# Turning probability blocks ahead, summing head norms in four 32-row strips, and moving a convolution and a state load in a hybrid decoder step

## The reference

```python
x += 0.5 * swiglu(rmsnorm(x)); x += mixer(rmsnorm(x)); x += 0.5 * swiglu(rmsnorm(x))   # per layer
# layer 0, mixer = [forgetting attention, 4 heads of 128 | gated DeltaNet, 4 heads of 128]
s = q @ k.T * scale + c_i - c_j; p = softmax(causal(s)); o = p @ v            # prompt; samples read a paged cache
c = silu(causal_conv(u, w))              # 12 chunks of 128 channels: q 4, k 4, v 4; four taps
q = l2norm(q) * 128 ** -0.5; k = l2norm(k)                                    # per head, over its 128 channels
M = tril_strict(k_beta @ k.T * gam) + I; X = solve(M, [v_beta, k_beta * exp(gc)])
v_new = u - w @ S; o = (q * exp(gc)) @ S + (q @ k.T * gam) @ v_new; S = S * exp(gl) + k_dec.T @ v_new
o = rmsnorm(o) * silu(z)
# layer 1, mixer = retention, 8 heads of 128 x 256: rope, decayed attention in 4 chunks, a state per sample token
```

## Time and profile before

| | us |
|---|---|
| time of the three runs, median (lowest to highest) | 2624.53 (2623.72 to 2630.95) |
| the profiled execution, its own time | 2619.68 |
| its span, first to last instruction | 2617.9 |
| PE busy (95% of the span) | 2497.5 |
| POOL / DVE / ACT busy | 1682.8 / 1269.6 / 566.7 |
| mean granted TensorE clock | 0.977 |
| attention heads and convolution | about 620 to 690 |
| norm of q and k | about 690 to 715 |
| DeltaNet pairs | about 715 to 864 |
| closing norm and gate | about 864 to 897 |
| retention turns | about 1709 to 2116 |

### The profile page before, as it was taken

The page is one execution under the profiler, slowest core; times in us unless marked ns, Lnnn a source line. Parts: engine busy times, 40 slices in busy tenths (PEclk is TensorE's granted clock), DMA queues, the critical chain, the costliest instruction groups (busy, mean ns, idle before and its releaser), DMA issues.

```text
span 2617.9 us, 53417 instructions
## 1 busy us (share of the span) xinstructions
PE 2497.5 (95%) x20047; PEld 2395.9 (92%) x20047; DVE 1269.6 (48%) x2225; ACT 566.7 (22%) x847; POOL 1682.8 (64%) x750
## 2 busy tenths in 40 slices
PE   7999998997789899999999999999999899999997
PEld 7999998995467799999999999999889799999996
DVE  4444335786333564443344443366766644444433
ACT  3222101004633222220022220022222221222101
POOL 5777775663411377777777777765545457777773
PEclk9999999998789899999999999999999999999998
DMA  4333334894375333333323333233333423333331
GB/s 125 90 89 96 101 79 113 285 308 131 84 220 188 85 89 95 89 88 99 118 81 89 95 91 100 82 91 100 116 116 98 126 81 88 89 95 90 96 93 61
DMA packets 472390, 291.19 MB, mean 111 GB/s; under 512 B 32785, under 2 KB 438411, under 8 KB 472270
## 3 DMA queue, kind: packets, MB, share of 16 engines
q1 hardware_dynamic: 407286, 221.15, 29.0%
q10 hardware_dynamic: 64992, 68.54, 8.4%
HBM read 273.50 MB, written 16.23 MB: 111 GB/s over the span
## 4 chain that ended last, share of the span: by engine, by line
PE 83%; DVE 8%; ACT 3%; issue 3%; DMA 1%; POOL 1%; ACTq 1%; DVEq 0%; SPq 0%; POOLq 0%
PE ACC L799 72%; PE ACC L1055 2%; PE ACC L1028 1%; DVE TB L2261 1%; DMA SSR<-in_state_ret_S 1%; DVE SSR L2178 1%; POOL WLO L708 1%; PE ACC L1306 0%; PE ACC L1296 0%; DVE XL L1736 0%; PE ACC L1122 0%; PE ACC L1037 0%; POOL WHI L705 0%; PE ACC L893 0%; PE ACC L1330 0%
## 5 line engine op out<-in xcount | busy, mean ns | idle before, releaser
L705 POOL TENSOR_TENSOR WHI<-RAW,ZERO 128x1024 fp32r<-128x1024 f32 (+1 forms) x341 | 693.0, 2032 | 677.2 <-PE ACC L799 640.3
L708 POOL TENSOR_TENSOR WLO<-RAW,WHI 128x1024 fp32r<-128x1024 f32 (+1 forms) x341 | 915.5, 2685 | 49.3 <-POOL WHI L705 2.3
L799 PE MATMUL ACC<-XH,WHI 128*128 128x260 f32 x4032 | 822.6, 285 | 4.3 <-DVE XL L1736 2.0
L799 PE MATMUL ACC<-XH,WLO 128*128 128x260 f32 x4032 | 813.7, 283 | 0.0
L799 PE MATMUL ACC<-XL,WHI 128*128 128x260 f32 x4032 | 812.4, 283 | 0.0
L799 PEld LDWEIGHTS ACC<-XH,WHI 128*128 128x128 f32 x4032 | 624.8, 189 | 22.9 <-issue 6.5
L799 PEld LDWEIGHTS ACC<-XH,WLO 128*128 128x128 f32 x4032 | 622.9, 189 | 0.0
L799 PEld LDWEIGHTS ACC<-XL,WHI 128*128 128x128 f32 x4032 | 621.6, 189 | 0.0
L799 PE MATMUL ACC<-HH,WHI 128*128 128x260 f32 x1408 | 284.2, 283 | 1.1 <-POOL WLO L708 1.1
L799 PE MATMUL ACC<-HH,WLO 128*128 128x260 f32 x1408 | 283.1, 282 | 0.0
L799 PE MATMUL ACC<-HL,WHI 128*128 128x260 f32 x1408 | 282.6, 282 | 0.0
(11 more groups left out here) (391 smaller groups left out, 2398.7 us busy)
## 6 DMA issues: line engine op xcount, KB each, us to landing
RAW<-in_ffn_w_gu SPq DMA_DIRECT2D x176, 512.0 KB, 3.9
RAW<-in_ffn_w_down SPq DMA_DIRECT2D x64, 704.0 KB, 4.8
KPAGES<-in_cache_fox_k ACTq DMA_DIRECT2D x128, 256.0 KB, 4.1
RAW<-in_c_w_in SPq DMA_DIRECT2D x48, 512.0 KB, 3.9
VPAGES<-in_cache_fox_v SPq DMA_DIRECT2D x72, 256.0 KB, 3.1
RAW<-in_ab_w_in SPq DMA_DIRECT2D x28, 512.0 KB, 5.4
VPAGES<-in_cache_fox_v ACTq DMA_DIRECT2D x56, 256.0 KB, 3.3
SSR<-in_state_ret_S ACTq DMA_DIRECT2D x8, 1024.0 KB, 5.4
```

What stands on the lines that cost most here:

```text
L705: pool.tensor_tensor(WHI[:, slot, 0:nk, :], RAW[:, slot, 0:nk, :], ZERO[:, :].broadcast_to([P, nk, P]), ALU.add).then_inc(hi_split, 1)
L708: pool.tensor_tensor(WLO[:, slot, 0:nk, :], RAW[:, slot, 0:nk, :], WHI[:, slot, 0:nk, :].bitcast(F32), ALU.subtract).then_inc(split, 1)
L799: ins = pe.matmul(ACC[acc][:, n, 0:HALF], w[:, slot, k, :], a[:, k0 + k, n * HALF:(n + 1) * HALF], start=first and opens, stop=final and c ...
```

## The change

The diff does five things.

- **Heads.** PE turns blocks 0 and 1 of a head first, and then, behind the value product of block q, turns block q+2. The turn of the next head's keys stands ahead of the two turns, that of its values behind them. ACT moves the high part of head h-1 into head h, takes `exponent(h, 3)` at the head's start, and places its three `conv_taps` between the copies. DVE takes the low part of head h-1 and the first maximum of head h+1 ahead of `normalize(h, 3)`.
- **Value convolution.** Chunks 9 to 11 leave the last head and stand on ACT behind the root of the norm. Silu of v stands in the first DeltaNet pair behind the scaled keys, with its own semaphore `cv_value`, for which PE waits before it turns v; Silu of z stands behind the root of the closing norm, with `cv_gate`.
- **Norm sums.** Squares of q are taken by DVE, those of k by ACT in two parts. The sums go to one bank, each (q or k, half) in a strip of 32 rows by 260 columns; root and reciprocal work on 128 rows by 260 columns (RN); a broadcast reads one strip. Two `values()` stand ahead of the sums and two behind, in place of four behind. The closing norm goes the same way, its sums in the order of heads 0, 2, 1, 3.
- **First pair's end.** `value_sum(1)` stands ahead of `sample_gates`; PE takes both corner products ahead of the two `values()`.
- **Retention.** The load of SSR, with its wait for the store, stands ahead of `swap(1, "k")`.

```diff
-        fb_pe = Steps(sem("fb_pe"), [f"{w}{q}" for q in range(NBLK) for w in ("turn", "pv")])
+        fb_pe = Steps(sem("fb_pe"), [f"{w}{q}" for q, w in ((0, "turn"), (1, "turn"), (0, "pv"), (2, "turn"), (1, "pv"), (3, "turn"), (2, "pv"), (3, "pv"))])
...
             for h in range(FOX_HEADS):
-                if 0 < h < FOX_HEADS - 1:
-                    fox_tokens(h + 1)
+                later = 0 < h < FOX_HEADS - 1
+                if later:
+                    fox_token_turn(h + 1, AB_K, "ktok")
+                fox_turn(h, 0)
+                fox_turn(h, 1)
+                if later:
+                    fox_token_turn(h + 1, AB_V, "vtok")
                 for q in range(NBLK):
-                    fox_turn(h, q)
                     if h + 1 < FOX_HEADS:
                         score(h + 1, q)
...
                     fox_values(h, q)
-
-            pe.wait_ge(fb_dve.sem, fb_dve.value("lo", FOX_HEADS - 1))
+                    if q + 2 < NBLK:
+                        fox_turn(h, q + 2)
...
+            for _ in range(V_SLOTS // 2):
+                values()
             for j in range(2 * GDN_HEADS):
...
-                    ins = pe.matmul(ACC[0][0:NORM_ROWS, n, 0:HALF], row_select(r), SQH[:, j, n * HALF:(n + 1) * HALF],
-                                    start=j == 0, stop=j == 2 * GDN_HEADS - 1)
+                    ins = pe.matmul(bank(0)[strip(2 * (j // GDN_HEADS) + n), 0:HALF], row_select(j % GDN_HEADS), SQH[:, j, n * HALF:(n + 1) * HALF],
+                                    start=j % GDN_HEADS == 0, stop=j % GDN_HEADS == GDN_HEADS - 1)
             ln_pe.done(ins, "sum")
-            for _ in range(V_SLOTS):
+            for _ in range(V_SLOTS // 2):
                 values()
...
+                    rows, r = strip(2 * (j // GDN_HEADS) + n), 32 * (2 * (j // GDN_HEADS) + n) + j % GDN_HEADS
+                    ins = pe.matmul(ACC[1 + j % 2][:, n, 0:HALF], IDENT[rows, r:r + 1].broadcast_to([32, P]), RN[rows, :], start=True, stop=True)
...
                 values()
+                pe.wait_ge(cv_value, 1)
                 for q in range(2):
                     await_step(pe, gl_act, f"kde{q}", p)
                     turned(q, GV, f"vt{q}")
...
                 corner_xt(0)
+                corner_xt(1)
                 values()
-                corner_xt(1)
                 values()
...
+            for h in range(FOX_HEADS):
+                last = h == FOX_HEADS - 1
+                if h > 0:
+                    if not last:
+                        fox_query(h + 1)
+                    fox_high(h - 1)
+                    if not last:
+                        fox_keys(h + 1)
+                fox_turned(h, 0)
+                fox_turned(h, 1)
+                if h > 0:
+                    exponent(h, 3)
+                if not last:
+                    conv_taps(3 * h)
+                    fox_turned(h, 2)
+                    exponent(h + 1, 0)
+                    exponent(h + 1, 1)
+                    conv_taps(3 * h + 1)
+                    fox_turned(h, 3)
+                    exponent(h + 1, 2)
+                    conv_taps(3 * h + 2)
+                else:
+                    fox_turned(h, 2)
+                    fox_silu(0)
+                    fox_silu(1)
+                    fox_turned(h, 3)
+                    fox_silu(2)
+                    fox_silu(3)
+                    fox_high(h)
...
-            ln_act.done(act.activation(SQH[:, 0:GDN_HEADS, :], channels(GQ, GDN_HEADS), ACT.Square), "sqq")
-            ln_act.done(act.activation(SQH[:, GDN_HEADS:, :], channels(GK, GDN_HEADS), ACT.Square), "sqk")
-            act.wait_ge(cv_pool.sem, cv_pool.value("add3", CONV_CH - 1))
-            act.activation(channels(GV, 2 * GDN_HEADS), channels(GV, 2 * GDN_HEADS), ACT.Silu).then_inc(cv_act, 1)
+            for n in range(2):
+                ln_act.done(act.activation(SQH[:, GDN_HEADS + 2 * n:GDN_HEADS + 2 * n + 2, :], channels(GK + 2 * n, 2), ACT.Square), f"sqk{n}")
...
+                ln_act.done(act.activation(RN[rows, :], bank(0)[rows, 0:HALF], ACT.Sqrt, bias=EPSC[rows, c:c + 1], scale=scale), name)
+            for c in range(3 * (FOX_HEADS - 1), CONV_CH):
+                conv_taps(c)
             act.wait_ge(ln_dve.sem, ln_dve.value(f"mul{2 * GDN_HEADS - 1}"))
...
+                if p == 0:
+                    act.wait_ge(cv_pool.sem, cv_pool.value("add3", CONV_CH - 1))
+                    act.activation(channels(GV, GDN_HEADS), channels(GV, GDN_HEADS), ACT.Silu).then_inc(cv_value, 1)
...
                     if p == 0 and n == LEVELS - 1:
+                        value_sum(1)
                         sample_gates()
...
-                if p == 0:
-                    value_sum(1)
...
+            go_act.done(act.activation(RN, bank(0)[:, 0:HALF], ACT.Sqrt, bias=EPSC[:, 0:1], scale=1.0 / P), "std")
+            act.activation(channels(AB_Z, GDN_HEADS), channels(AB_Z, GDN_HEADS), ACT.Silu).then_inc(cv_gate, 1)
...
+                if not is_first:
+                    hold(act, rss_stored, 16 * g + 16, 16)
+                    act.dma_start(SSR[:, :, :], state_ret[0][:, bass.ds(g, 1)].rearrange("b a k v -> k b (a v)")).then_inc(rss_in, 16)
                 if not is_last:
                     swap(1, "k")
...
+                if h > 0:
+                    await_step(dve, fb_act, "hi", h - 1)
+                    fb_dve.done(dve.tensor_tensor(MOL[:, h - 1, 0:SEQ], bank(VALUE_BANK), MOH[:, h - 1, 0:SEQ].bitcast(F32), ALU.subtract), "lo")
+                    if h + 1 < FOX_HEADS:
+                        fox_value_tokens(h + 1)
+                if h + 1 < FOX_HEADS:
+                    row_max(h + 1, 0)
                 normalize(h, 3)
...
+            dve.wait_ge(cv_act, 2)
+            q = PRJ[:, GQ:GQ + GDN_HEADS, :]
+            ln_dve.done(dve.tensor_tensor(SQH[:, 0:GDN_HEADS, :], q, q, ALU.mult), "sqq")
...
-            ln_dve.done(dve.reciprocal(TA[0:NORM_ROWS, :], TA[0:NORM_ROWS, :]), "inv")
+            ln_dve.done(dve.reciprocal(RN, RN), "inv")
```

100 lines of the change are left out of this document (47 added, 53 removed).

## The result

The changed kernel takes 2584.74 us, median of four runs (2579.71 to 2586.60), against 2624.12 for the kernel before, whose runs lie between 2621.32 and 2630.95. The ratio is 0.9843, with a 95% interval from 0.9819 to 0.9868: 39.4 us faster, inside the predicted range and less than 0.1 us from the predicted time. A second series gave 2580.34 (2578.79 to 2586.35) against 2618.66, ratio 0.985 (0.9836 to 0.9864). The sum was right; its terms were not, and that the median hits it so closely is luck. The two profiled executions of the changed kernel have spans of 2584.8 and 2584.5 us, 33.1 and 33.4 less than the 2617.9 of before.

What follows compares the result with a forecast made beforehand. Projections, 72% of the span, stay untouched; between them ACT's waits bound the heads, single steps the norm, PE the levels. Stage gains less the Silu of v loss sum to 39.8 us: 2624.5 − 39.8 = 2584.7, range 2571 to 2605.

Steps and rivals of the forecast that it cites:

- Heads 0 to 2: First three heads: the new order covers most of ACT's waits; gain 11.9 us, bounds 6 and 14.5.
- half of the waits stay: Head 0: about half of ACT's waits remain, as DVE's chain moves back some 1.5 us; gain taken as 3.5 us.
- Norm up to the roots: From MOH's end to the roots' end: sums in strips go from 10.0 to 5.0 us; gain 4.5, bounds −0.5 and 7.9.
- all at 2.4 GHz: Upper bound of the norm up to the roots, gain 7.9 us, where the squares of k end last.
- Roots to EG: Roots to the first pair's Exp: three conv_taps and the Exp table take 20.8 us to 19.2; gain 1.6.
- bring nothing here: Roots to the first Exp: DVE's 10.3 us is covered by ACT's 10.5, so shorter reciprocal and strip broadcasts gain nothing.
- Silu of v: First pair: table load and Silu ahead of VB make PE wait; loss 3.0 us, bounds 2.5 and 3.2.
- rival 3: Levels of both pairs: PE idles for Silu of v, clock falls to 1.2 GHz, 35 us become 70 twice; 2654.7 us, 4%.
- Pair's end: End of the first pair: value sum ahead of the gates; gain 6.0 us, bounds 5.3 and 6.7.
- both go: First pair's end: PE's 4.46 us wait for the value sum and the two value turns' 1.2 GHz clock both disappear; 6.4 us.
- Closing norm: Closing norm: earlier, shorter reciprocal gives 3.0 us and strip broadcasts 3.6; gain 6.6, bounds 3.0 and 6.6.
- Retention: Retention: SSR loaded earlier, so PE's two waits for it go; gain 4.1 us, bounds 2 and 5.

## Why the prediction was right, point by point

**Heads 0 to 2: mechanism right, size between 9.1 and 11.7 for 11.9.** The order is worth 6.6 to 9.2 us in these heads and 11.3 to 11.6 up to the roots, shown by undoing it. Head 0 gave 1.5 and 2.7 for 3.5. The step that failed is "half of the waits stay" there: it let the later sum put DVE's chain back by some 1.5 us, where DVE waited 2.33, and left out that the chain then meets POOL's additions. That DVE's small products get some six times longer beside POOL was weighed only at `normalize`; the rows here (1.14 for 0.19) agree with what the Trainium skill, "SBUF — State Buffer", section "Who interferes with whom", says of operations with two inputs in SBUF.

**Head 3: right,** 7.7 and 7.1 for 8.1.

**Norm up to the roots: term too small, 9.1 and 7.5 for 4.5.** The step that failed in both profiles is the sums: 10.0 was halved for two strips at a time, from a length at a mixed clock. In one block they take 7.23 at 2.4 GHz, and in strips 2.8, not 5.0; half of 7.23 would be 3.6, and what makes the rest was not tried. PE also started 1.3 us ahead of MOH's end and not 0.5. The value turns, counted at 1.2 GHz (3.7 us), ran at 2.4 in the first profile (1.90) and as counted in the second (3.55), which is the 1.6 between the two. The bound "all at 2.4 GHz" is the case of the first profile, and was still too low: from MOH's end to that of the roots there are 4.3 us, all of them ACT's (squares 2.02, table 1.28, roots 0.97), and PE's sums lie beside them.

**Roots to EG: 2.7 for 1.6.** The three conv_taps and the Exp table came as worked out (EGC 10.8 us behind the roots, worked out as 10.5). One of eight page issues ran during the table load, which gave 1.5. The sentence that the shorter reciprocal and the broadcasts from strips "bring nothing here" holds for the sum (DVE's products end 9.3 us behind the roots, ACT's EGC starts at 10.8), and yet rests on a price at 2.4 GHz: without strips the same broadcasts take 13.47 us here, and the stage takes 26.5 us in place of 18.1, 5.7 more than before the change.

**Silu of v: −5.5 for −3.0.** The table load and the Silu cost nearly what they were put at (1.28 and 1.94 for 1.28 and 1.83). Two steps failed. The turn of v starts 3.7 us later against EG and not 3.0: the 0.3 that was taken off is ACT's wait ahead of VB, and it doesn't go, since PE's first turn of v, which ran beside ACT's scaled keys, now stands behind the Silu (ACT waits 1.21, and 0.75 with the clock kept up). And rival 3 on a small scale was left out: PE's wait of 5.25 us lets the clock fall, and the EG product of level 1 comes 1.8 us later behind the turn. The 20 matmuls in the wait show it, since they give this 1.8 back. The clock came back with the levels (0.99 from 715 to 750), so the rival's large price was rightly held improbable. The drain that the Trainium skill, "ScalarE: Activation LUTs", section "What ACT_TABLE_LOAD costs", adds to each switch does not show here: load and Silu follow the activations ahead of them within 0.02 us.

**Pair's end: 3.6 for 6.0,** with 7.7 where the clock held. The step "both go" was half right: the wait goes, worth 3.0 by itself, and the turns at 1.2 GHz go only in some executions. The step took the low clock for a consequence of the wait; in the trace of before it had fallen ahead of the wait (the row at 772.44), and after the change it falls although PE is busy throughout (35.00 of 35 us from 715 to 750, then 10.00 of 10).

**Closing norm: 5.0 and 5.3 for 6.6.** The reciprocal started 0.26 us earlier and not 1.1, since the products of the value sums ran 5.74 in place of 4.99; reciprocal and broadcasts gave 4.7 of the 5.3 counted for them.

**Retention: 5.2 and 3.7 for 4.1,** mechanism shown; with the load in its old place the waits made 7.0 us in another execution, so the bound of 5 was too narrow.

**What was not in the sum:** −1.5 ahead of the heads and −2.7 and −1.5 behind the closing norm. Behind the closing norm the granted clock is 0.50 from 866 to 870, and the records of the fifth chunk take 0.64 us where they took 0.41 before, at 1.00; ahead of the heads the small products of PE are longer in the same way (1.55 us at 612.29 for eight records, 1.06 before, with the clock at 0.67 and 1.00 from 612 to 614). Both are the clock, but for 0.5 of the 1.5: ACT's copy of the tails (610.69 and 610.16) is already late by that, at a clock of 1.00 in both kernels, and the cause of it is open.

The median came out as forecast because a term that was 4.6 too small stood against two that were off the other way by some 2.5 (Silu of v, pair's end), one by 1.6 (closing norm), one by 2.8 (heads 0 to 2) and losses of the clock, and because the frame, the median of before, was itself a draw: it was 2624.1, 2621.2, 2622.6 and 2618.7 in four series. The gain from profile to profile was 33.1 and 33.4, not 39.8. The low ends of the forecast's bounds add up to 19.6 and the high ends to 48.3, not to 19.3 and 48; nothing hangs on it.

## What to carry to other kernels

Price a step that puts a wait ahead of TensorE by two rows, the wait and the work behind it at half its clock: 5.25 us of waiting cost another 1.8 here, and packing matmuls into strips paid most where the one-block form started at half the clock (13.47 us of broadcasts). When an instruction is moved on one engine, follow the small ones that now stand behind it: a sum of 0.5 us put off by one turn cost DVE 2.3 us and then a meeting with POOL. And undo each named part by itself: the convolution's move, forecast at 6.7, was worth 1 to 2, while the strips of the two norms, put at 8 to 10, were worth 16.

## What the runs showed of the hardware that was not expected

- The granted clock is not a function of the program alone. The same kernel took 45.6 us for heads 0 to 2 in one profile (0.88 from 635 to 649) and 43.0 in another (1.00), and 1.90 and 3.55 us for the same two value turns. With the same order of instructions the end of the first pair took 40.6 us in some executions, at a clock of 1.00, and 43 to 45 in others, at about half for most of the corner and the value turns.
- An activation table load did not hold up ACT's DMA issues here: one page load was issued at 688.53, within the table load of 688.00 to 689.28.
- Matmuls into four different 32-row strips of one bank took 0.25 us each (eight in 1.96 us) at a clock of 0.50, where in one block of rows they took 0.59 at 0.78 in the closing norm of before.
- A product of two small tiles on DVE (128 by 32) took 0.19 to 0.22 us alone and 1.14 to 1.32 beside POOL's additions.
